# Two stretches of unread identity matmuls on TensorE, in front of the first expert item's rows and in front of the gathered expert rows

## The reference

```python
logits = jnp.dot(xt.astype(jnp.float32), w_router.astype(jnp.float32))
top_v, top_i = lax.top_k(logits, TOP_K)
top_w = jax.nn.softmax(top_v, axis=-1)
order = jnp.argsort(top_i.reshape(-1));  tok = order // TOP_K
xs = xt[tok]
h = jax.nn.silu(lax.ragged_dot(xs, wg, sizes)) * lax.ragged_dot(xs, wu, sizes)
ys = lax.ragged_dot(h, wd, sizes) * top_w.reshape(-1)[order][:, None]
y = jnp.zeros_like(xt).at[tok].add(ys)
...
x = x + f
g = jax.nn.sigmoid(jnp.einsum('bld,de->ble', _rmsnorm(x, ...), W['ple_w_gate'][i]))
x = x + g * jnp.einsum('blp,pd->bld', p[i], W['ple_w_proj'][i])
```

## Time and profile before

| | |
|---|---|
| time, median of 3 runs | 5141.82 us (5138.27 to 5151.62) |
| the profiled execution | 5149.72 us |
| mean granted TensorE clock | 0.977 of 2.4 GHz |
| DVE busy, ACT busy, POOL busy | 66%, 31%, 8% of the span |

### The profile page before, as it was taken

One profiled execution on the slowest core, in us unless ns is written; L12 is line 12 of the kernel. 1 busy time (PEld: TensorE's weight loads), 2 busy tenths in 40 slices (PEclk: granted clock), 3 DMA queues, 4 the chain that ended last, 5 costly groups with the idle time before them and its releaser, 6 DMA issues. The chain is left out here.

```text
span 5148.1 us, 86753 instructions
## 1 busy us (share of the span) xinstructions
PE 4943.8 (96%) x33110; PEld 4879.4 (95%) x33111; DVE 3396.1 (66%) x5288; ACT 1597.9 (31%) x2290; POOL 394.1 (8%) x239
## 2 busy tenths in 40 slices
PE   8999999999999999999959999999999999999968
PEld 8999999999998999999959999999999999999958
DVE  5677756444556756866557777666668777876665
ACT  2112122111113311122224444333334444443333
POOL 3111101111002121110010000000000000000020
PEclk9999999999999999999979999999999999999989
DMA  3111111111111111111035454444446555654431
GB/s 105 44 45 42 41 40 43 48 41 49 41 46 40 42 54 48 40 40 42 28 126 184 164 185 164 161 139 162 154 152 200 185 194 180 203 178 147 147 116 42
DMA packets 398850, 527.79 MB, mean 103 GB/s; under 512 B 11944, under 2 KB 353494, under 8 KB 398504
## 3 DMA queue, kind: packets, MB, share of 16 engines
q1 hardware_dynamic: 359552, 460.75, 27.1%
q0 software_dynamic: 10912, 33.94, 2.0%
q10 hardware_dynamic: 28040, 28.63, 1.7%
HBM read 494.87 MB, written 28.39 MB: 102 GB/s over the span
## 5 line engine op out<-in xcount | busy, mean ns | idle before, releaser
L1571 DVE TENSOR_TENSOR WLO<-WRAW,WHI 128x1024 fp32r<-128x1024 f32 x866 | 1071.1, 1238 | 344.6 <-ACT WHI L1167 221.2
L657 PE MATMUL PS<-XHI,WHI 128*128 128x384 f32 (+1 forms) x3648 | 1202.5, 330 | 10.6 <-DVE XLO L1818 4.5
L659 PE MATMUL PS<-XHI,WLO 128*128 128x384 f32 (+1 forms) x3648 | 1196.9, 328 | 0.0
L658 PE MATMUL PS<-XLO,WHI 128*128 128x384 f32 (+1 forms) x3648 | 1196.4, 328 | 0.0
L1167 ACT ACTIVATE WHI<-WRAW 128x1024 fp32r<-128x1024 f32 x866 | 899.2, 1051 | 890.1 <-PE PS L772 605.9
L657 PE MATMUL PS<-XSH,WHI 128*128 128x232 f32 (+6 forms) x3584 | 1058.1, 295 | 8.6 <-DVEq L2275 6.7
L659 PE MATMUL PS<-XSH,WLO 128*128 128x232 f32 (+6 forms) x3584 | 1054.5, 294 | 0.0
L658 PE MATMUL PS<-XSL,WHI 128*128 128x232 f32 (+6 forms) x3584 | 1053.5, 294 | 0.0
L657 PEld LDWEIGHTS PS<-XHI,WHI 128*128 128x128 f32 x3648 | 691.1, 189 | 13.0 <-issue 5.2
L658 PEld LDWEIGHTS PS<-XLO,WHI 128*128 128x128 f32 x3648 | 690.9, 189 | 0.9
L659 PEld LDWEIGHTS PS<-XHI,WLO 128*128 128x128 f32 x3648 | 690.3, 189 | 0.0
(11 more groups left out here) (361 smaller groups left out, 5957.8 us busy)
## 6 DMA issues: line engine op xcount, KB each, us to landing
WRAW<-in_moe_w_gate SPq DMA_DIRECT2D x112, 1024.0 KB, 5.0
WRAW<-in_moe_w_up SPq DMA_DIRECT2D x112, 1024.0 KB, 5.0
WRAW<-in_moe_w_down SPq DMA_DIRECT2D x112, 1024.0 KB, 4.9
WRAW<-in_w_in SPq DMA_DIRECT2D x48, 1024.0 KB, 5.2
WRAW<-in_ffn_w_gate SPq DMA_DIRECT2D x11, 1024.0 KB, 5.2
WRAW<-in_ffn_w_up SPq DMA_DIRECT2D x11, 1024.0 KB, 5.3
WRAW<-in_ffn_w_down SPq DMA_DIRECT2D x11, 1024.0 KB, 5.0
XG<-sorted_rows POOLq DMA_DIRECT2D x18, 512.0 KB, 4.8
```

The source lines that it names most:

```text
L657: pe.matmul(PS[:, bank, 0:n], wh, hi(k), start=(k == 0), stop=False)
L658: pe.matmul(PS[:, bank, 0:n], wh, lo(k), start=False, stop=False)
L659: ins = pe.matmul(PS[:, bank, 0:n], wl, hi(k), start=False, stop=(k == KC - 1))
L1571: v.do(dve.tensor_tensor(WLO[s][:], raw_view(conv.n // 2 % RAW, conv.n % 2, kind), WHI[s][:].bitcast(F32), ALU.subtract), conv)
```

## The change

A helper takes the next `misc` bank without counting it as used, and writes the product of the identity IDR and 384 columns of XHI to it `count` times. Nobody reads it; the next use of that bank overwrites it. It is called with 130 behind the load of `extras` and in front of the loop over extra items, and with 64 behind the last `item_out` and in front of the pass over the token tiles.

```diff
                             ins = pe.transpose(PS[0:n, b, k * P:(k + 1) * P], EACC[:, 4 * h + k, r0:r0 + n], IDF[:])
                         ins.then_inc(m.next(), 1)
 
+                def turn_over(count):
+
+                    b = misc_bank()
+                    for _ in range(count):
+                        pe.matmul(PS[:, b, 0:384], IDR[:], XHI[:, 0, 0:384], start=True, stop=True)
+
+                turn_over(130)
                 last = MOE_GROUPS - 1
 
                 def gate_up(rows, splits=None):
@@ -1098,6 +1105,7 @@
                 q_item = q.at(q.n)
                 for j in range(len(XBLK)):
                     item_out(j)
+                turn_over(64)
                 for j in range(NT):
                     n = tokens(j)
                     pe.wait_ge(S["combined"], j + 1)
```

## The result

Over 20 runs each the changed kernel takes 5153.88 us (5147.1 to 5165.58), the kernel before 5143.06 us (5130.31 to 5157.53): a ratio of 1.0023, 95% interval 1.0014 to 1.0031. The medians lie 10.8 us apart, the ratio stands for 11.8 us (7 to 16 us): small, but clear of no change. Forecast were 5148 us and a ratio of 1.0012, 6.1 us.

The account below looks back on a forecast made before the run. PE, busy 96% of 5148.1 us, was taken to bound the kernel. 5149.72 us + 6.5 - 0.4 = 5155.8 us, a ratio of 1.0012, or 5148 us on the median of 5141.82 us; range 5138 to 5157 us.

Parts of the forecast that it names:

- PE bounds, and the waits are others' work: Whole kernel: PE is busy 96% of 5148.1 us; both waits, 29.97 and 16.47 us, are not PE's to shorten.
- The first burst fits the wait by itself: Wait before L969: 130 matmuls take 24.4 us and end at 2685.6, just as L969 starts; no cost by the array alone.
- The sequencer leaves it early and only then does the loop: Wait before L969: sequencer hands over the last matmul 3.0 us early, then runs the loop; L969 starts 6.5 us late.
- The jump, 4.7 us: Loop over extra items, L1028: its one long jump takes 4.7 us, the middle; lower end 0.42 us, upper 5.87 us.
- The delay reaches the end one for one: Behind the first wait: PE idles little apart from jumps, so the 6.5 us delay reaches the end in full.
- Nothing is given back: First wait: PE is idle again before L969, so L969 and the first L657 keep their low-clock price.
- The second burst, -0.4 us: Before the token tiles, L1108: 64 matmuls cost 0 and make the first group 0.4 us earlier, ends 0 and 1.5 us.
- The rival of the clock that stays up: Both waits: the clock stays up and nothing is late, giving 5136 us; chance 0.07.
- the prize that I had priced at 4.3 us at the first wait: First wait, at the high clock: 2.2 us from the 24 transposes and 2.1 us from the 15 matmuls.
- The rival of the moved code: L1023: the added instructions make the other four jumps long, 20 us on top of the forecast, 5168 us; chance 0.06.
- The terms' own upper end: First wait: +8.5 us, with a jump of 5.87 us and a somewhat longer low-clock stretch.

Follow-up runs that it names:

- the narrow burst: One burst of 130 matmuls of 160 columns behind the loop over extra items, no second burst, against the kernel before: 5152.75 us, ratio 1.0017.

## Why the prediction was right, point by point

- **PE bounds, and the waits are others' work**: right. No run got the rows sooner: they land 42.4 to 44.5 us behind POOL's first scatter in all of them, before 43.1 us.
- **The first burst fits the wait by itself**: its length is right, 24.70 us for 24.4 (25.44 and 24.52 in the other two profiles), its end was put with no slack. It ended 0.8, 2.0 and 1.7 us after the time at which the rows would have let L969 start, and the sum had 0 for that.
- **The sequencer leaves it early and only then does the loop**: right, and the heart of the case. The lead was 2.9 us to the last matmul's start (3.0 counted out). By D, L969 came 5.1 and 5.6 us late in the changed kernel's two profiles and 6.5 us with the first burst alone, against 6.5 us forecast; by the rows' landing 5.8, 7.0 and 7.3 us. That the forecast lies among these is in part luck: it is 5.0 to 5.4 us of loop behind the burst and 0.8 to 2.0 us of a late end, where the forecast had 6.5 us and 0. With 40 it was not late, with 200 it was 17.0 us, and behind the loop (66) 1.0 us, all of that waited for the DMA.
- **The jump, 4.7 us**: mis-sized by 1.0 to 1.2 us. It took 3.45, 3.73, 3.72 and 3.70 us in the four runs in which it came near the end of the wait, and 3.46 to 7.89 us in the others, where DMAs mostly ran beside it. The value that I had from L1095 (3.46 us) would have been right.
- **The delay reaches the end one for one**: not shown more closely than the scatter allows. With 200 in front, 17.0 us at L969 and 3.3 us at the first L657 stand beside 23 us (15 to 28 us); with the narrow burst 14 us stand beside 10 us (4 to 13 us).
- **Nothing is given back**: right. The first L657 ran at the low clock and G stayed 12.2 us.
- **The second burst, -0.4 us**: within its ends, and not to be told from 0. In the changed kernel the clock fell during the 5.24 us that PE still waited.
- **The rival of the clock that stays up**: it failed as put. The Trainium skill's rule ("TensorE: Matmul & The Clock Gate", "Why this matters for your kernels") agrees in part: with wide matmuls up to and between the transposes, PE had no long gap and the transposes ran at the high clock. But with 66 behind the loop PE had no idle time over 2.52 us from the burst through the transposes either, and the clock fell (0.56 over them); the absence of long gaps was not enough. And the prize that I had priced at 4.3 us at the first wait was 1.2 us there. ACT's and DVE's parts and PE's register work stand between the transposes whatever the clock, and the clock fell just behind them.
- **The rival of the moved code**: at its place, L1023, nothing shows that the added code matters. But the mechanism is real at another place that I had not looked at, the alignment in front of `item_begin`: 3.0 us. The changed kernel, whose code moves by 260 instructions, has the short jump in both profiles.

What stays open is size. The terms' own upper end was 8.5 us, and the time lies inside the stated range only by what that range held for scatter. The changed kernel was measured twice, 1.0023 and 1.0026, some 11 to 13 us, nearly double the 6.1 us forecast; its profiles place 5.8 and 7.0 us of that at the first wait and show no other place where the bursts delay PE. The first burst alone gave 1.0011 (up to 1.0023), the second alone 0.9996. Either the long jumps at L1023 come more often with both bursts (each adds some 5 us; of the three items where they change, the changed kernel's profiles had 1 and 3 long ones, before had 2), or the run with one burst fell low by scatter. It would take many profiles of the changed kernel to say, and there are two.

## What to carry to other kernels

Filler in a wait is not free because the engine is idle: ask what stands between the filler and the wait in program order, above all jumps, and put the filler behind them, directly ahead of the wait. Leave slack: a wait also takes in what comes late ahead of it, and a filler that fills it to the end hands that on. Then ask what the engine does first after the wait; where it works in short pieces between other engines, a high clock at its start is worth less than one jump. And where code is aligned to blocks, look at the jumps before comparing variants whose code is shifted differently, since instructions that never run made one jump of this kernel 3 us longer.

## What was not expected of the hardware

- Matmuls of 160 columns, back to back for 28 us, were granted 0.50 throughout and took 0.215 us each; those of 384 columns had the clock up after 3 to 6 us and took 0.174 us. The Trainium skill, "TensorE: Matmul & The Clock Gate", section "The HAM clock gate (the "warmup" mystery)", says that activity releases the throttle; PE was busy 27.92 of 28.00 us here and the clock stayed low. The measurement decides, and no run here shows why.
- Long jumps held PE's sequencer for 3.3 to 7.9 us, and the jump at L1023 of the same item was under 0.8 us in one execution and 5.5 us in another. PE's idle time before L770, of which each long one makes some 5.8 us, was 11.4 to 28.5 us, the largest scatter that PE's waits show; the time up to POOL's first scatter, ahead of the change, varies by 12 us as well (2636.2 to 2648.2).
